# Interleaving the two column blocks of a weight slot, and moving three norm tiles, in a one-core transformer kernel

## The reference

```
p = rms_norm(h, g) @ w_in                 # every product: 256 x 1024 times 1024 x n
q = (xn @ w_q); k = (memn @ w_k)          # cross attention
qh = xb @ w_pq                            # queries of the expert layer
u, v = split(hn @ w_up, 2)                # feed-forward, width 2 x 2816, in both layers
out = (silu(conv(u)) * v) @ w_down
```

## Time and profile before

| what | value |
|---|---|
| three runs | 1668.18, 1668.85, 1672.76 us |
| median | 1668.85 us |
| span of the profiled execution | 1670.5 us, at a granted clock of 1.000 |
| TensorE busy with products / with loads | 99% / 92% of the span |
| VectorE, ScalarE, GpSimd busy | 74%, 56%, 15% |

### The profile page before, as it was taken

How to read it: one execution, slowest core, us unless ns; L and a number is a source line. 1 busy time by engine, 2 the same in 40 slices (tenths; PEclk the granted TensorE clock), 3 DMA queues, 4 the chain that set the end, 5 groups by cost and what they waited for, 6 DMA issues and landing times.

```text
span 1670.5 us, 30280 instructions
## 1 busy us (share of the span) xinstructions
PE 1652.9 (99%) x12006; PEld 1542.5 (92%) x12006; DVE 1237.3 (74%) x1896; ACT 935.2 (56%) x1139; POOL 242.8 (15%) x333
## 2 busy tenths in 40 slices
PE   8999999999999999999999999999999999999999
PEld 8999999999999999988888888999999888899987
DVE  6875467999998666667676676887888565769974
ACT  7885565555546555545555454786545357565542
POOL 0000000004667676211010110000000000100000
PEclk9999999999999999999999999999999999999999
DMA  7445344776555555777777776533555544345553
GB/s 304 152 152 180 120 159 157 231 233 213 189 178 191 190 189 191 270 240 238 245 235 239 241 238 222 221 133 139 184 185 195 180 174 152 124 156 203 200 188 115
DMA packets 73804, 323.40 MB, mean 194 GB/s; under 512 B 8663, under 2 KB 9047, under 8 KB 55744
## 3 DMA queue, kind: packets, MB, share of 16 engines
q1 hardware_dynamic: 58736, 285.18, 50.1%
q0 software_dynamic: 5568, 19.38, 3.7%
q10 hardware_dynamic: 9360, 16.92, 2.7%
HBM read 303.62 MB, written 17.83 MB: 192 GB/s over the span
## 4 chain that ended last, share of the span: by engine, by line
PE 83%; DVE 12%; ACT 4%; issue 1%; DMA 0%; SPq 0%; ACTq 0%; DVEq 0%
PE bank L605 14%; PE bank L606 13%; PE bank L607 13%; PE bank L986 7%; PE bank L985 7%; PE bank L987 7%; PE bank L938 5%; PE bank L942 5%; PE bank L941 5%; DVE lo_u L2299 3%; PE bank L950 2%; DVE wlo L1914 2%; DVE oh L2310 1%; ACT whi L1350 1%; DVE pos L2196 1%
## 5 line engine op out<-in xcount | busy, mean ns | idle before, releaser
L1586 ACT ACTIVATE hi_u<-raw_u 128x1024 fp32r<-128x1024 f32 x256 | 271.8, 1062 | 279.6 <-PE bank L985 165.2
L1914 DVE TENSOR_TENSOR wlo<-raw,whi 128x2048 fp32r<-128x2048 f32 (+1 forms) x141 | 314.7, 2232 | 105.6 <-PE bank L605 83.3
L1350 ACT ACTIVATE whi<-raw 128x2048 fp32r<-128x2048 f32 x137 | 263.1, 1920 | 77.6 <-PE bank L605 74.7
L938 PE MATMUL bank<-xh,hi_u 128*128 128x256 f32 x1024 | 291.9, 285 | 1.5 <-DVE lo_u L2299 1.2
L2299 DVE TENSOR_TENSOR lo_u<-raw_u,hi_u 128x1024 fp32r<-128x1024 f32 x192 | 237.9, 1239 | 70.4 <-PE bank L938 62.4
L941 PE MATMUL bank<-xl,hi_u 128*128 128x256 f32 x1024 | 285.4, 279 | 0.0
L942 PE MATMUL bank<-xh,lo_u 128*128 128x256 f32 x1024 | 285.3, 279 | 0.0
L605 PE MATMUL bank<-nh,whi 128*128 128x256 f32 x904 | 253.4, 280 | 0.5 <-DVE wlo L1914 0.4
L607 PE MATMUL bank<-nh,wlo 128*128 128x256 f32 x904 | 251.9, 279 | 0.0
L606 PE MATMUL bank<-nl,whi 128*128 128x256 f32 x904 | 251.9, 279 | 0.0
L519 POOL TENSOR_SCALAR oh<-kept,sel_T 128x128 f32<-128x128 f32 x256 | 199.9, 797 | 249.3 <-ACT sel_T L1636 166.4
(11 more groups left out here) (417 smaller groups left out, 3358.7 us busy)
## 6 DMA issues: line engine op xcount, KB each, us to landing
raw<-in_weights SPq DMA_DIRECT2D x138, 1024.0 KB, 4.8
raw_u<-in_experts SPq DMA_DIRECT2D x256, 512.0 KB, 4.2
aside<-a_out ACTq DMA_DIRECT2D x64, 256.0 KB, 3.6
a_in<-aside POOLq DMA_DIRECT2D x64, 256.0 KB, 3.7
const<-in_const SPq DMA_DIRECT2D x1, 1409.0 KB, 9.0
const<-in_const POOLq DMA_DIRECT2D x1, 1409.0 KB, 6.4
h<-in_x SPq DMA_DIRECT2D x2, 512.0 KB, 5.1
raw<-in_weights SPq DMA_DIRECT2D x2, 512.0 KB, 7.6
```

The source lines that it names most:

```text
L938: mm = pe.matmul(out, w[0][:, kp], xh[:, k, :], start=(k == 0), stop=False)
L1350: a(A(whi[:, n % HIGH, :], raw[:, n % RAW, :], ACT.Copy), S("weights_hi"))
L1586: a(A(hi_u[:, u % HIGH_U, :], raw_u[:, u % RAW_U, :], ACT.Copy), S("unit_high"))
L1914: v(V.tensor_tensor(wlo[:, n % LOW, place], raw[:, n % RAW, place], whi[:, n % HIGH, place].bitcast(F32), ALU.subtract), S("weights_split" ...
```

## The change

The host stores a T slot with its two column blocks interleaved: for each `k`, word `2j + c` holds column `j` of block `c`. The load of a column block then reads 128 words at every second place, over 256 words, where before it read 128 words in a row. `columns(p, k, c)` is the access pattern, in all three places that make T products. N slots stay as they were, and the splits, which take whole slots, don't change. Besides, three norm tiles move: `nh1` from -16 to -32, `nh5` from -16 to -64, `nh7` from -16 to -96. `xh` and `memh`, which T stages use too, stay at -16, since N stages use them as well.

```diff
-        p3.beside(HIGH_AT, -16)
+        p3.beside(HIGH_AT, -32)
...
-        for n_, by in ((4, 16), (5, -16), (6, 16), (7, -16)):
+        for n_, by in ((4, 16), (5, -64), (6, 16), (7, -96)):
...
+            def columns(p, k, c):
+
+                return p[:, k, :].rearrange("p (n c) -> p c n", c=2)[:, c, :]
...
             def outs_T(bank):
-                return [(bank[:, c * T:(c + 1) * T], lambda w, src, k, c=c: [p[:, k, c * P:(c + 1) * P] for p in w],
+                return [(bank[:, c * T:(c + 1) * T], lambda w, src, k, c=c: [columns(p, k, c) for p in w],
...
-                    mm = three(out, [p[:, k, c0:c0 + P] for p in w], [x[:, k, :] for x in src], k == 0, k == KD - 1)
+                    mm = three(out, [columns(p, k, c0 // P) for p in w], [x[:, k, :] for x in src], k == 0, k == KD - 1)
...
+    def slots_T(w):
+
+        return [s.reshape(P, KD, 2, P).transpose(0, 1, 3, 2).reshape(P, -1) for s in slots(w)]
...
-        return slots(np.concatenate([np.concatenate([w[:, a:a + P], w[:, f + a:f + a + P]], 1) for a in range(0, f, P)], 1))
+        return slots_T(np.concatenate([np.concatenate([w[:, a:a + P], w[:, f + a:f + a + P]], 1) for a in range(0, f, P)], 1))
...
-    ws = (slots(w_in) + slots(one("w_xk")) + w_xv[0:1] + slots(w_out) + w_xv[1:2] + slots(one("w_xq")) + w_xv[2:4]
+    ws = (slots_T(w_in[:, :1536]) + slots(w_in[:, 1536:]) + slots_T(one("w_xk")) + w_xv[0:1] + slots(w_out) + w_xv[1:2] + slots_T(one("w_xq")) + w_xv[2:4]
```

More of the change, by code:

```diff
@@ L705, in _ @@
                     for k in range(4 * half, 4 * half + 4):
-                        mm = three(bank[:, c * T:(c + 1) * T], [p[:, k, c * P:(c + 1) * P] for p in w], [x[:, k, :] for x in xn],
+                        mm = three(bank[:, c * T:(c + 1) * T], [columns(p, k, c) for p in w], [x[:, k, :] for x in xn],
                                    k == 0 and c == 0, k == KD - 1, True)
@@ L2730, in pack @@
     w_even = np.concatenate([w_even[:, 0:1024], w_even[:, 1536:3584], w_even[:, 1024:1536]], 1)
-    ws = (slots(w_in) + slots(one("w_xk")) + w_xv[0:1] + slots(w_out) + w_xv[1:2] + slots(one("w_xq")) + w_xv[2:4]
-          + slots(one("w_xo")) + slots(one("w_pq")) + slots(w_even) + slots(g["even_w_out_2"][0])
-          + up(g["ffn_w_up_2"][0]) + down(g["ffn_w_down_2"][0]) + slots(w_odd[:, :256]) + slots(w_odd[:, 3072:]) + slots(w_odd[:, 256:3072])
+    ws = (slots_T(w_in[:, :1536]) + slots(w_in[:, 1536:]) + slots_T(one("w_xk")) + w_xv[0:1] + slots(w_out) + w_xv[1:2] + slots_T(one("w_xq")) + w_xv[2:4]
+          + slots(one("w_xo")) + slots_T(one("w_pq")) + slots(w_even) + slots(g["even_w_out_2"][0])
+          + up(g["ffn_w_up_2"][0]) + down(g["ffn_w_down_2"][0]) + slots(w_odd[:, :256]) + slots_T(w_odd[:, 3072:]) + slots(w_odd[:, 256:3072])
           + slots(g["odd_w_out_2"][0]) + up(g["ffn_w_up_2"][1]) + down(g["ffn_w_down_2"][1]))
```

## The result

The changed kernel takes 1683.35 us (median of three runs, 1682.52 to 1683.54) against 1668.85; the ratio is 1.0083, 95% interval 1.0066 to 1.0099. It is slower by 14.5 us, and lies outside the forecast range of 1650 to 1678.

What follows compares the result with a forecast made beforehand. The prediction took the pace of 3168 T products, with two paces seen, as what the change affects: the 1670.5 us span less 7.3 us lost against the faster pace gave 1663.2 us, with an 8-in-10 range of 1650 to 1678.

Steps and rivals of the forecast that it cites:

- The slack of a load: In fast T stretches, a load has at most a few ns to spare within 113; growth beyond is paid 3168 times.
- rival (d): All of T with nh1, nh5, nh7: stepped loads lengthen or always meet the moving stream, costing 6.8 to 9.5 us; chance 0.22.
- The last of the signs of being wrong: T's pace taking a third value above 118 ns would mean the step costs the load itself, unbounded by the trace.
- fast pace in all of T: Every T product at the faster of two paces seen, 113.3 against 117.7 ns, winning 7.3 us: 1663.2 us.
- the forecast (a): All T stages: streams that keep their distance hold the faster pace seen, 113.3 ns a product; 1663 us, chance 0.33.
- the 3 ns of the fp32 rows: Plain fp32 products, streams in step: 275 ns at distance 0 modulo 32, 272 at 16, taken as a meeting's price.
- The 6.8: Cost in us if all T triples run at the slower pace seen, 13.2 ns more a triple; 1677.3 us.
- The 9.5: Cost in us if 3 ns come on top of the present mix for each of 3168 T products; 1680.0 us.
- The sum: Whole kernel: span of 1670.5 us less 7.3 us lost in T against its faster pace, giving 1663.2 us.
- the 12.7 us of the sum: Further win if all 3168 T products fell from 276 to 272 ns, 4 ns each; lower bound 1650.5 us.
- rival (b): All of T: the streams stop disturbing each other altogether, products last 272 ns; 1650 us, chance 0.20.
- (c): T stages: restart phase picks the pace, the change only rethrows it, 4.6 us per up stage; 1664 to 1675, chance 0.25.

Runs made afterwards that it cites:

- e3: Kernel before, with up0 and up1 making each T product in two halves of 128 tokens, contiguous loads; 1887.67 us.
- e1: Changed kernel with the norm tiles back at distance -16, so only the stepped load remains; 1681.82 us against 1667.91 for the kernel before, ratio 1.0072.
- e7: Changed kernel, stepped loads kept, with nh1 at distance 0, nh5 at 16 and nh7 at 48; 1682.49 us.
- e4: Changed kernel, with up0 and up1 making each T product in two halves of 128 tokens, stepped loads; 1916.59 us.
- g1: Changed kernel with 128-token halves in up0 (distance -16) and up1 (0), and stepped gated-tile loads in down0 (64) and down1 (112); 1916.14 us.
- g2: Kernel before with contiguous 128-token halves, nh1 at -32, nh5 at -64, nh7 at -96, gated tiles at 96 and 0; 1890.70 us.
- e5: Kernel before, with down0 and down1 loading the gated tile's columns at a step of two, distance still 80; 1678.99 us against 1672.19.
- e2: Kernel before, contiguous loads, with only the three norm tiles moved to -32, -64 and -96; 1680.94 us, ratio 1.0066.
- f4: Kernel before, contiguous loads, with gated tiles at 64 (down0) and 112 (down1) instead of 80, and nh1, nh5, nh4 at 16; 1674.64 us.
- e6: Changed kernel with four column blocks interleaved instead of two, so a load reads every fourth word; 2048.63 us.
- f1: Kernel before, contiguous loads, with nh1 at -24, nh5 at -8, nh7 at 8 and, in N stages, nh4 at 40, nh6 at 56; 1680.58 us.
- f2: Kernel before, contiguous loads, with nh1 at 24, nh5 at 48, nh7 at 80 and, in N stages, nh4 at 88, nh6 at 72; 1676.55 us.

## Why the prediction was wrong

**What stood.** The kernel is bound by TensorE's pace (99% busy, 83% of the chain before and 86% after), and the growth is in the 3168 T products, 13.2 us in the traces. The slack of a load (a few ns) and the point from which rival (d) decides, about 3 ns, were nearly right: 113.3 less the 111.7 of e3 leaves 1.6 ns, the load grew by 6.4 alone, and a product with it went to 120 ns. The last of the signs of being wrong, a third pace above 118 ns, is what came.

**The step that failed** is the choice of "fast pace in all of T", the forecast (a), on the ground that streams that pass the same number of words keep their distance and so don't disturb each other. Under the step T has 120 ns at six distances and 121.1 at the seventh (e1, e7, after), so keeping step wins nothing at any of them. In its place stands: with loads setting the pace, beside half as many moving columns, a stepped load costs 6.1 to 6.4 ns a product (e3, e4, g1, g2), and at distance 80 it slows a stream of 512 columns that has ample room for it (e5, 3.7 ns). The step alone, at the old distance, costs 13.9 us (e1).

**The term that was mis-sized** is the price of a load with a step. I bounded it by the 3 ns of the fp32 rows; measured 6.4 ns alone, and 20.3 ns a triple over the fast pace in whole products. Rival (d) had 6.8 to 9.5 us for it, against 14.1 by the same way of counting, or 13.2 summed over the two traces. The 6.8 took the slow pace as the worst there is, and the range ended at 1678, with that case. The 9.5 took the 3 ns. The sum also started at 1670.5, the span of an execution that was the slowest of the three: with the 1.8 us around the span that is about 3.5 us over the median.

**Readings that misled.** From two paces at one distance I concluded that the pace isn't set by the distance alone. That is so, the distance doesn't choose between 113.3 and 117.7 ns at -16; but -16 was the only distance in T that the trace had. At -64 and -96 the pace is 120 ns (e2), at -8 118.3. The three new distances alone cost 13 us. The fp32 rows, 275 ns at 0 modulo 32 against 272 at 16, had hinted that 0 is a bad class; I took it as a price of streams in step only and never put it on the contiguous load. For 512 moving columns the class doesn't carry over (f4: 228.0 ns at 64, 233.3 at 112). And a duration doesn't tell the pace across kernels, as I had taken from two stretches of one trace: 281 ns stood for 117.7 there, but in e1 `up1` has 280 ns at a pace of 119.9, and in f4 `up0` has 279 at 117.8. Only start to start tells it.

**The floor.** T doesn't go under 113 ns: no run has a T product of 256 columns with a shorter pace over a stretch, none shows the 4 ns a product behind the 12.7 us of the sum, and rival (b), 1650 us at a chance of 0.20, had more than it deserved. Of (c), the dice, the part that is true is the spread of the kernel before: 1665.72 to 1673.47 us in 17 runs on one chip; `up0` was slow and `up1` fast in the profile before. With the step every traced execution has the one pace of about 120 ns, and the three runs of the changed kernel agree to 1 us. Rival (d), at a chance of 0.22, was on the right side, but too low in its price, and too narrow in its place: it had only the stages with `nh1`, `nh5` and `nh7`, and `in` and `xk`, at the old distance, went to 120 ns too.

**Load and moving stream together.** The two streams don't go independently of each other: a product takes 113.3 or 117.7 ns in the kernel before and 120.0 or 119.9 in `up0` and `up1` of e2, where only tiles were moved. A step of two costs a load about 6 ns where loads set the pace (e3, e4), and with a step of four a product takes 237 ns (e6).

**What stays open.** Why the step's cost and the distance's cost don't add, but end at the same 120.0 ns, isn't shown. What picks the slow or the fast pace at a restart wasn't found either, nor why beside 512 columns the step costs 5.3 ns at 64 and 3.7 at 80 and gains 2.8 at 112. That it is the distance of two tiles and not their own addresses is argued above, and no run moved both together.

## What to carry to other kernels

When TensorE is bound by pairs of a load and a product, measure the start-to-start distance of a long stretch before anything else, and treat the moving tile's address less the loaded tile's, modulo 128 words, as a parameter that is scanned on the chip: it was worth 6% of a stage (113.3 against 120.0 ns). Don't buy a new distance or a better phase with a step in the load: a step of two cost 6 ns a load and one of four doubled the product (237 ns). Change layout and addresses in separate runs: here each of the two cost nearly all of it alone (13.9 and 13.0 us of 14.5), and one can hide the other.

## What the runs showed of the hardware

- Loads of 128 fp32r columns set a pace of 111.7 to 111.9 ns contiguous (e3, g2), 118.0 to 118.1 with a step of two (e4, g1), at the distances tried; with a step of four a product takes 237 ns (e6).
- Products of 256 fp32r columns with contiguous loads, by distance: 113.3 or 117.7 ns at -16, 48 and 16 (one or the other for a whole stretch), 117.7 at 80, 116.7 at 8, 118.3 at -8, 120.0 at -64 and 119.9 at -96. In `xq`, over 21 us each: 118.6 at -24 (f1), 120.1 at 24 (f2), 118.4 at -32 (e2).
- Products of 512 columns, contiguous: 227.6 ns at 0, 228.0 at 64, 229.6 at 80, 233.3 at 112; 96 gave 56.0 / 80 / 3 = 233.3. With stepped loads: 233.3 at 64 and 80, 230.5 at 112.
- A pace once taken is held for hundreds of products without a break (317 slow triples in `up0` of before, 316 fast in `up1`), and can be another after a restart (`nh1`: 64 triples slow, 48 fast, 46 slow); that is 4.6 us for an `up` stage here, against a spread of 7.8 us between the runs of the kernel before. That such changes make most of this spread is likely, but not shown: only one execution of it has a trace.
